# Rounded products for layer 0's xBC projection in a two-layer hybrid diffusion step, and what is moved around them

## The chip, the core and the metric

The kernel runs on one core of one Trainium2 chip. The metric is the device time of one execution in microseconds (us). Five engines work side by side: TensorE (PE; its weight loads are PEld), VectorE (DVE), ScalarE (ACT), GpSimd (POOL) and SyncE (SP), which issues the loads. Each works through its own list of instructions in order and waits only on semaphores.

## The reference, cut to what matters

128 context and 256 latent tokens (384 together) of width 1024 pass through two trunk layers. What the change touches is the first half of a layer: an RMS norm with a modulation, and one input projection whose columns go to attention A, attention B, a gate z, the part `xbc` (768 columns) and `dt` (16 columns, padded to 32).

```python
h = modulate(rmsnorm(x, n1), sh1, sc1)          # sh1, sc1 = slices of silu(c) @ w_ada + b_ada
a_q, a_k, a_v, b_q, b_k, b_v, z, xbc, dt_raw = jnp.split(h @ w_in, points, axis=-1)
xbc = jax.nn.silu(conv_centred(xbc, conv_w, conv_b))
dt = softplus(dt_raw + dt_bias)                  # the scan's decays come from dt
```

Then follow the two attentions, the state-space scan on xbc and dt, an output projection, and a mixture of 16 experts.

## The kernel before

Activations lie transposed, channels on partitions, in 8 chunks k of 128 channels by 384 tokens. Weights stream through a ring of 8 slots of 1 MB; SP issues their loads in one fixed order (`pieces`), and before each it waits until the slot's former piece is used up (`release`). The order of the work is written out by hand in `layer_steps`: every engine walks the same list of steps and does its own part of each.

**A product in parts.** A full fp32 product is one matmul in the source and two matmul records in the trace. A rounded product splits both operands into a high part (rounded to fp32r) and a low part (the rest) and sums three fp32r matmuls: high x high, high x low, low x high. ACT makes a high part by a copy, DVE the low part by a subtraction. The experts, the output projection, the row stage below and layer 1's xbc (`ROUNDED = (1,)`) work so; layer 0's xbc uses full fp32 products.

**Layer 0's front.** The modulation of layer 0 is not there yet, so its columns come in eight pieces `first(0..7)` of 1 MB. For each chunk j, PE multiplies (`first`, L755), ACT copies the result to `ada_rows` (L1572), PE turns it (`first_turn`, L766), and DVE adds the bias and gain (L1840, L1842) and modulates chunk j of the normalised x (L1903). Then PE multiplies chunk k of h with the six column blocks of xbc (L981). Within chunk k, PE does `first_turn(k + 1)` after block 1 and `first(k + 2)` after block 4. In chunks 3 and 7, four thin products for dt come first (L963); in chunk 7 DVE copies their sum to `tmp` (L2083; in a rounded layer it is L2088), and PE waits for that copy at `dt_rows` behind block 2 (L780).

**The pieces of xbc's weights** are ("xbc", l, 0) to ("xbc", l, 3), two chunks each. Where a layer is rounded, ACT makes `wx_hi` (`x_split`, L1425; two buffers, so pieces 2 and 3 wait until chunks 1 and 3 are multiplied) and DVE makes the rest in place (`x_rest_split`, L1938). The high part of h, `hT_hi`, lies over ring slots 2 and 3; in layer 0 those slots hold xbc pieces 1 and 0 first, and h is split late (`h_split`: ACT L1595, DVE L1943).

**Behind the front** comes the row stage: tokens by 512 columns (L1014), parts p = 0 to 5 of w_in, each split by ACT and DVE (`split_win`, L1416 and L1933). Beside it run the convolution (ACT L1607, DVE L2097 to L2102), Silu (L1620), dt's softplus on DVE (L2110 to L2142, which ends with `da_lo` and `dtd`), and `masked_rest(0)`: 16 ACT instructions at L1431 which need `da_lo`. They stand as step ("rest", 0) behind the Silus and before the first copies of row results (L1639, L1641). PE needs those copies to get its PSUM banks back.

**Layer 1's front** has three pieces of adaLN weights ahead of xbc (`early = 3`; PE L704) and three more behind the row stage (`burst`). DVE makes the rest of x's piece 1 before it scales x by the norm (L1862); `parts_of(c)` makes each chunk's fp32 form h_f (L1871) and its low part (L1876), ACT its high part (L1488).

## Time and profile before

| | |
|---|---|
| median of 3 runs | 789.55 us (788.98 to 789.73) |
| the profiled execution | 789.94 us, of which its span is 788.0 us |
| busy: PE, PEld, DVE, ACT, POOL | 742.7, 576.4, 582.8, 502.6, 50.4 us |
| layer 0's front, up to the row stage | 0 to 62.1 us |
| layer 0's row stage | 62.1 to about 135 us |
| layer 1's front, up to the row stage | about 406 to 444.7 us |

The page of the profile has busy times, the span in slices, the chain of work that ended last, and groups of instructions. A timeline's row has the start in us, the length in us, the engine, the source line, the operation, out<-in, shape and count, and in brackets the idle time before it and what ended it. Merged rows (x2, x16) run from the first start to the last end. A matmul's own length includes its drain, so the pace of a stream is read from a run of many.

### The profile page before, as it was taken

Reading aid. Unit: us, or ns where it says so; the run is one execution under the profiler, and the core shown is the slowest. Engines: PE = TensorE matmul, PEld = TensorE weight load, DVE = VectorE, ACT = ScalarE, POOL = GpSimd, SP = SyncE. Lnnn points to the kernel's source line nnn. Section 1 sums busy time; section 2 is a strip of 40 time slices with the busy share of each in tenths; the row PEclk is TensorE's granted clock in tenths of the full one; section 3 lists DMA queues with packets and bytes.
Section 4 is the critical chain, followed back from the end, with each engine's and each line's share of the span. In section 5 each row is a group of like instructions: output and inputs, shape, how many; then the busy total and the mean of one; then the engine's idle time right before and its main releaser. Section 6 shows DMA issues by size and latency. Waiting matters only on the chain.

```text
span 788.0 us, 10974 instructions
## 1 busy us (share of the span) xinstructions
PE 742.7 (94%) x4020; PEld 576.4 (73%) x4020; DVE 582.8 (74%) x968; ACT 502.6 (64%) x834; POOL 50.4 (6%) x36
## 2 busy tenths in 40 slices
PE   4999999899999999999989999989999999999994
PEld 2557777457976888888769888745698788888874
DVE  3258377886656889999868646869676789999965
ACT  3047784484466877777646488557556787777752
POOL 0001342000000000000000035200000000000000
PEclk9999999999999999999999999999999999999998
DMA  9963033978328899999843112386741189999902
GB/s 363 423 237 108 1 133 116 424 274 309 109 107 340 318 377 362 377 376 361 308 181 146 67 54 70 119 362 216 283 153 56 54 319 363 374 364 379 372 17 83
DMA packets 33489, 186.26 MB, mean 236 GB/s; under 512 B 5136, under 2 KB 6288, under 8 KB 16400
## 3 DMA queue, kind: packets, MB, share of 16 engines
q1 hardware_dynamic: 33424, 185.42, 62.4%
q8 instruction: 37, 0.61, 0.3%
q14 instruction: 28, 0.23, 0.1%
HBM read 182.79 MB, written 2.62 MB: 235 GB/s over the span
## 4 chain that ended last, share of the span: by engine, by line
PE 70%; DVE 13%; ACT 10%; issue 5%; DMA 1%; DVEq 0%; ACTq 0%; SPq 0%
PE psum L874 22%; PE psum L903 11%; PE psum L1014 7%; PE psum L1216 5%; PE psum L981 4%; PE psum L926 3%; PE psum L704 3%; PE psum L978 3%; PE psum L852 2%; DVE att L2250 1%; ACT ud L1431 1%; PE psum L755 1%; DVE xbc L2097 1%; ACT split L1407 1%; ACT ring_r L1416 1%
## 5 line engine op out<-in xcount | busy, mean ns | idle before, releaser
L2039 DVE TENSOR_TENSOR split<-ring,split 128x2048 fp32r<-128x2048 f32 x96 | 219.9, 2290 | 26.8 <-ACT split L1532 25.4
L1532 ACT CAST split<-ring 128x2048 fp32r<-128x2048 f32 x96 | 183.5, 1912 | 21.9 <-PE psum L903 14.5
L874 PE MATMUL psum<-split,y_hi 128*128 128x512 f32 x512 | 160.8, 395 | 0.4 <-ACT selT L1505 0.4
L874 PEld LDWEIGHTS psum<-split,y_hi 128*128 128x128 f32 x512 | 93.7, 188 | 18.6 <-issue 0.5
L874 PE MATMUL psum<-split,y_lo 128*128 128x512 f32 x256 | 100.1, 391 | 0.0
L1014 PE MATMUL psum<-ring_r,hT_hi 128*128 128x512 f32 x216 | 74.2, 398 | 1.4 <-ACT row L1641 1.4
L903 PE MATMUL psum<-split,hidT 128*128 128x512 f32 x256 | 69.7, 394 | 1.8 <-DVE hidT_lo L2044 1.8
L903 PEld LDWEIGHTS psum<-split,hidT 128*128 128x128 f32 x256 | 47.3, 188 | 14.2 <-DVE hidT_lo L2044 4.8
L874 PEld LDWEIGHTS psum<-split,y_lo 128*128 128x128 f32 x256 | 48.1, 188 | 10.2
L2480 POOL TENSOR_TENSOR ud<-const,da_hi 128x1024 fp32r<-128x1024 f32 x12 | 27.3, 2294 | 404.2 <-DVE da_lo L2141 397.3
L1014 PEld LDWEIGHTS psum<-ring_r,hT_hi 128*128 128x128 f32 x216 | 40.6, 191 | 10.9 <-issue 2.4
L1445 ACT ACTIVATE row<-xT 128x384 f32<-128x384 f32 x40 | 20.2, 520 | 32.8 <-DVE xT L1950 29.9
L1706 ACT ACTIVATE hT<-psum,att 128x384 f32<-128x384 f32 (+1 forms) x48 | 24.0, 507 | 26.7 <-DVE att L2260 18.6
L704 PE MATMUL psum<-ring,silu_c 128*32 128x512 f32 x320 | 39.9, 600 | 0.0
L903 PE MATMUL psum<-split,hidT_lo 128*128 128x512 f32 x128 | 39.5, 390 | 0.0
L1950 DVE SCALAR_TENSOR_TENSOR xT<-psum,mods,xT 128x128 f32<-128x128 f32 x64 | 23.7, 413 | 20.7 <-PE psum L1216 15.3
L981 PE MATMUL psum<-hT,ring 128*128 128x384 f32 x96 | 35.3, 502 | 0.0
L1216 PE MATMUL psum<-m_hi,split 128*128 128x384 f32 x128 | 34.4, 337 | 0.0
L1216 PE MATMUL psum<-o_hi,split 128*128 128x384 f32 x128 | 33.7, 336 | 0.0
L1538 ACT CAST hidT<-psum 128x256 fp32r<-128x256 f32 x32 | 12.0, 374 | 28.8 <-PE psum L887 28.8
L1014 PE MATMUL psum<-ring_r,hT_lo 128*128 128x512 f32 x72 | 28.8, 400 | 0.0
L1431 ACT ACTIVATE ud<-const,da_lo 128x128 fp32r<-128x128 f32 x96 | 28.7, 393 | 0.0
(308 smaller groups left out, 1431.5 us busy)
## 6 DMA issues: line engine op xcount, KB each, us to landing
ring<-in_w_gu SPq DMA_DIRECT2D x64, 1024.0 KB, 5.2
ring<-in_w_ada SPq DMA_DIRECT2D x40, 1024.0 KB, 6.9
ring<-in_w_down SPq DMA_DIRECT2D x32, 1024.0 KB, 5.3
ring<-in_w_rows SPq DMA_DIRECT2D x12, 1024.0 KB, 4.8
ring<-in_first SPq DMA_DIRECT2D x8, 1024.0 KB, 14.6
ring<-in_w_out SPq DMA_DIRECT2D x8, 1024.0 KB, 5.2
ring<-in_w_xbc SPq DMA_DIRECT2D x8, 800.0 KB, 8.3
par<-in_par SPq DMA_DIRECT2D x1, 1728.0 KB, 13.3
```

Source lines behind the costliest of these rows:

```text
L704: last = pe.matmul(psum[32 * q:32 * q + 32, 7, :], silu_c[:, k, :], w[:, q * 512:(q + 1) * 512], start=(k == 0), stop=(k == KD - 1), skip_ ...
L874: last = pe.matmul(dst, x[:, g, t, :], w[:, j, :], start=(t == 0 and i == 0), stop=(t == KD - 1 and i == 2))
L903: last = pe.matmul(psum[:, b, :], x, w[:, half * 512:(half + 1) * 512], start=(e % EPG == 0 and i == 0), stop=(e % EPG == EPG - 1 and i == ...
L981: last = pe.matmul(bank(("xbc", l, c))[:, 0:TOK], w[:, kk, c * P:(c + 1) * P], hT[:, k, :], start=(k == 0), stop=(k == KD - 1))
L1014: last = pe.matmul(dst, x[:, k, tok], w[:, j, :], start=(k == 0 and i == 0), stop=(k == KD - 1 and i == 2))
L1216: last = pe.matmul(dst[:, 0:TOK], w[:, k, cols], x[:, k, :], start=(part == 1 and k == 0 and i == 0), stop=(part == 0 and k == 3 and i == 2))
L1431: ins = act.activation(ud[:, 1, d, h, :], c_(tri), ACT.Copy, scale=da_lo[:, m, SH * d + h:SH * d + h + 1])
L1532: act.copy(splits[unit_split(n)][:, 0, :], slot(key)).then_inc(raised("whi", l, p), 1)
L1706: act.activation(probs[:, u % 8, 0:w], src[:, 0:w], ACT.Exp, bias=att[:, 1, u:u + 1], scale=SCALE, accum_out=att[:, 2, u:u + 1]).then_inc( ...
L1950: ins = stt(xT[:, c, part], src[:, part], mods[:, l, gate + c, j:j + 1], xT[:, c, part], ALU.mult, ALU.add)
L2039: tt(lo, slot(unit_key(l, p, n)), hi.bitcast(F32), ALU.subtract).then_inc(raised("wlo", l, p), 1)
L2480: ins = tt(ud[:, 0, d, :, :], c_(tri).unsqueeze(1).to_broadcast((P, SH, P)), da_hi[:, m, 8 * d:8 * d + 8].bitcast(F32).unsqueeze(2).to_bro ...
```

## The change

It does these things:

- `ROUNDED = (0, 1)`: layer 0's xbc becomes three fp32r matmuls per product too. Chunk 0 is done high-part-of-h first, so that it waits for `hT_hi` alone; this holds for layer 1 as well.
- In layer 0, ACT's loop over j now holds: copy `ada_rows`, wait for chunk j's h_f, make its high part, and behind j = 0, 2, 4 `x_split` of piece 1, 2, 3. `split_win(0, 0)` and `(0, 1)` come behind the whole loop instead of behind j = 6.
- In layer 0, DVE scales x in groups (1, 1, 2, 4 chunks), modulates into `h_f`, makes each low part at once, and `x_rest_split` behind chunks 0, 2, 4. The rests of `split_win(0, 0)` and `(0, 1)` come behind the whole loop. The copy of dt's sum to `tmp` now stands in step xbc, behind them.
- `hT_hi` has ring slots 2 and 3 from the start of layer 0, so six slots are left for the first pieces. By the slot rule the load of first 4 waits for first 0, xbc 2 for first 1, first 5 for first 2, first 6 for first 3, xbc 3 for first 4, and first 7 for first 5; the parameters `par`, which `tables()` on DVE needs behind chunk 5, are issued behind first 7.
- The norm's factor goes to its own tile `rstd` instead of back to PSUM.
- `masked_rest(0)` moves between Silu 2 and Silu 3, in both layers; DVE's rest of `split_win(l, 2)` moves from the middle of dt's chain to behind the convolution.
- Layer 1: `early = 4`, so one adaLN piece moves from the burst to ahead of xbc; x's rest 1 on DVE moves from before the scaling to behind chunk 1's parts.

```diff
-ROUNDED = (1,)
+ROUNDED = (0, 1)
...
-    early = 3 if l else 0
+    early = 4 if l else 0
...
-    s += [("rows", 0, m) for m in range(TILES)] + [("rest", 0)] + [("rows", 1, m) for m in range(TILES)]
+    s += [("rows", 0, m) for m in range(TILES)] + [("rows", 1, m) for m in range(TILES)]
...
-    burst = early + 3
+    burst = 6 if l else 3
...
+        if key in (("xbc", 0, 0), ("xbc", 0, 1)):
+            last_use[b] = pieces.index(("first", 0, 5)) + 0.1 * (key[2] + 1)
...
                                 if l in ROUNDED:
+                                    h = h_f
+                                    if k == 0:
+                                        pe.wait_ge(*hx("hx_hi", l, 0))
+                                        for c in range(6):
+                                            cols = slice(c * P, (c + 1) * P)
+                                            pe.wait_ge(*fill(("xbc", l, c)))
+                                            for n, wp in enumerate((wx_hi[:, 0, 0, cols], x_lo_of(l, 0)[:, 0, cols])):
+                                                pe.matmul(bank(("xbc", l, c))[:, 0:TOK], wp, hT_hi[:, 0, :], start=(n == 0), stop=False)
                                     pe.wait_ge(*hx("hx_lo", l, k))
-                                    h = h_f
...
                         if not (l or arg[0]):
                             act.wait_ge(setup_dve, 1)
+                            x_split(0, 0)
...
                                 act.copy(ada_rows[:, 0:2 * P], bank(key)[:, 0:2 * P]).then_inc(*was_read(key))
-                                if j == KD - 2:
-                                    for p in range(2):
-                                        split_win(0, p)
+                                act.wait_ge(*modulated(0, 0, j))
+                                act.copy(hT_hi[:, j, :], h_f[:, j, :]).then_inc(sig["hx_hi"], 1)
+                                if j in (0, 2, 4):
+                                    x_split(0, 1 + j // 2)
+                            for p in range(2):
+                                split_win(0, p)
...
                             act.activation(xbc[:, c, :], xbc[:, c, :], ACT.Silu).then_inc(sig["xbc_silu"], 1)
+                            if c == 2:
+                                act.wait_ge(sig["da_lo"], per["da_lo"] * l + 1)
+                                masked_rest(0)
...
+                if not l:
+                    groups = {0: (0, 1), 1: (1, 2), 2: (2, 4), 4: (4, KD)}
+                    scaled(0, 1).then_inc(dve_step, 1)
+                    dve.wait_ge(dve_step, dve_steps())
+                    for c in range(KD):
+                        first(c)
+                        moved(c).then_inc(sig["h"], 1)
+                        if c + 1 in groups:
+                            scaled(*groups[c + 1]).then_inc(dve_step, 1)
+                            dve.wait_ge(dve_step, dve_steps())
+                        dve.wait_ge(*modulated(0, 0, c))
+                        rest_of(c)
+                        if c in (0, 2, 4):
+                            x_rest_split(0, 1 + c // 2)
+                        if c == KD - 3:
+                            tables()
+                    for p in range(2):
+                        split_win(0, p)
+                    return
                 if l in ROUNDED:
...
                     parts_of(1)
+                    x_rest_split(l, 1)
                     parts_of(2)
...
-                        split_win(l, 2)
                         dve.wait_ge(sig["dt_r"], per["dt_r"] * l + 1)
...
                         for c in range(3, 6):
                             side_taps(c)
+                        split_win(l, 2)
                         split_win(l, 3)
```

## Rows read from the trace of the kernel before

**Rows 1.** The page, part 1: busy us, share of the span, instructions.

```profile
PE 742.7 (94%) x4020; PEld 576.4 (73%) x4020; DVE 582.8 (74%) x968; ACT 502.6 (64%) x834; POOL 50.4 (6%) x36
```

**Rows 2.** The chain of waits in layer 0: start us, us, what.

```profile
20.07 2.04 PE psum L981 x6
...
27.63 1.00 PE psum L755 x16
...
56.83 0.83 PE psum L963 x8
...
125.25 8.20 PE psum L1014 x36
```

**Rows 3.** The chain of waits in layer 1.

```profile
426.74 12.79 PE psum L978 x72
...
515.83 2.71 PE psum L704 x24
```

**Rows 4.** Timeline of PE in layer 0.

```profile
19.57 0.50 PE L766 MATMUL psum<-pcol,ada_rows 128*128 128x2 f32 x4
...
59.58 0.74 PE L780 MATMUL psum<-pcol,tmp 128*128 128x16 f32 x6
...
62.14 0.47 PE L1014 MATMUL psum<-w_hi,hT_hi 128*128 128x512 f32 x1
```

**Rows 5.** Loads: SP's issue of xbc 1, its time to landing, and that of w_in's parts.

```profile
5.09 0.47 SPq L1323 DMA_DIRECT2D ring<-in_w_xbc  x1
...
ring<-in_w_xbc SPq DMA_DIRECT2D x1, 800.0 KB, 16.0
...
ring<-in_w_rows SPq DMA_DIRECT2D x12, 1024.0 KB, 4.8
```

**Rows 6.** Timeline of ACT in both layers.

```profile
15.62 0.37 ACT L1572 COPY ada_rows<-psum 128x256 f32<-128x256 f32 x1 [0.43 <-PE psum L755]
...
46.49 3.70 ACT L1416 CAST w_hi<-ring 128x2048 fp32r<-128x2048 f32 x2
...
76.63 4.79 ACT L1431 ACTIVATE ud<-const,da_lo 128x128 fp32r<-128x128 f32 x16
...
422.93 1.48 ACT L1425 CAST wx_hi<-ring 128x1536 fp32r<-128x1536 f32 x1 [0.44 <-PE psum L978]
```

**Rows 7.** Timeline of DVE in both layers' fronts.

```profile
25.63 0.16 DVE L1840 TENSOR_TENSOR mods<-psum,pcol 128x4 f32<-128x4 f32 x1 [3.65 <-PE psum L766]
...
26.09 0.67 DVE L1903 TENSOR_SCALAR hT<-hT,amul,mods 128x128 f32<-128x128 f32 x2
...
49.78 4.48 DVE L1933 TENSOR_TENSOR ring_r<-ring,w_hi 128x2048 fp32r<-128x2048 f32 x2
...
57.68 0.56 DVE L2083 COPY tmp<-psum 128x384 f32<-128x384 f32 x1 [0.70 <-PE psum L963]
...
409.96 1.76 DVE L1938 TENSOR_TENSOR ring_r<-ring,wx_hi 128x1536 fp32r<-128x1536 f32 x1 [3.43 <-issue]
...
413.86 0.95 DVE L1862 TENSOR_TENSOR hT<-xT,psum 128x768 f32<-128x768 f32 x1
...
417.08 1.75 DVE L1862 TENSOR_TENSOR hT<-xT,psum 128x1536 f32<-128x1536 f32 x1
```

**Rows 8.** Timeline of PE around layer 0's first row copies.

```profile
82.08 0.70 PE L1014 MATMUL psum<-ring_r,hT_hi 128*128 128x512 f32 x2 [1.12 <-ACT row L1641]
...
86.28 0.61 PE L1014 MATMUL psum<-w_hi,hT_hi 128*128 128x512 f32 x1
```

**Rows 9.** Timeline of PE in layer 1, around xbc's start and the row copies.

```profile
414.20 0.47 PE L978 MATMUL psum<-hT_hi,wx_hi 128*128 128x384 f32 x1 [3.08 <-DVE hT_lo L1876]
...
463.80 0.71 PE L1014 MATMUL psum<-ring_r,hT_hi 128*128 128x512 f32 x2 [0.28 <-ACT row L1641]
```

**Rows 10.** By windows: busy PE, PEld, DVE, ACT, POOL; granted clock; DMA.

```profile
80.00:85.00 5.00, 3.88 (x18) 3.18 (x18) 0.81 (x7) 5.00 (x17) 1.17 (x2) 0.83 0.00 0
...
415.00:420.00 5.00, 4.74 (x19) 4.42 (x19) 4.89 (x11) 2.85 (x7) 0.00 (x0) 0.72 0.22 92
```

More of the change, by code:

```diff
@@ L294, in build @@
                     pieces.append(("first", 0, 0))
-                for i in range(2 if l in ROUNDED else 0, KD // 2):
+                for i in range(2 if l else 0, KD // 2):
                     pieces.append(("xbc", l, i))
@@ L301, in build @@
             elif s[0] == "ada":
-                if s[2:] == (1, 0) and l in ROUNDED:
+                if s[2:] == (1, 0) and l:
                     pieces += [("xbc", l, 0), ("xbc", l, 1)]
@@ L357, in build @@
         last_use[b], last_key[b] = n, key
-    more_slots = [b for b in range(HELD, RING) if b not in [place["xbc", l, i] for l in ROUNDED for i in range(2)]]
+        if key in (("xbc", 0, 0), ("xbc", 0, 1)):
+            last_use[b] = pieces.index(("first", 0, 5)) + 0.1 * (key[2] + 1)
+    more_slots = [b for b in range(HELD, RING) if b not in [place["xbc", l, i] for l in ROUNDED if l for i in range(2)]]
     for l in range(DEPTH):
@@ L384, in build @@
         wx_hi = sb("wx_hi", [P, 2, 2, XBC], F32R)
+        rstd = sb("rstd", [P, TOK])
         with ExitStack() as shared:
@@ L971, in _ @@
                                 for c in range(6):
-                                    if k == 0:
+                                    if k == 0 and l not in ROUNDED:
                                         pe.wait_ge(*fill(("xbc", l, c)))
@@ L976, in _ @@
                                         hi, lo = wx_hi[:, i % 2, kk, cols], x_lo_of(l, i)[:, kk, cols]
-                                        for n, (wp, hp) in enumerate(((hi, hT_hi), (hi, hT_lo), (lo, hT_hi))):
+                                        for n, (wp, hp) in enumerate(((hi, hT_lo), (hi, hT_hi), (lo, hT_hi))[0:3 if k else 1]):
                                             last = pe.matmul(bank(("xbc", l, c))[:, 0:TOK], wp, hp[:, k, :],
-                                                             start=(k == 0 and n == 0), stop=(k == KD - 1 and n == 2))
+                                                             start=False, stop=(k == KD - 1 and n == 2))
                                     else:
@@ L1421, in x_split @@
                 if i == 2:
-                    act.wait_ge(sig["wx_spent"], ROUNDED.index(l) + 1)
+                    act.wait_ge(sig["wx_spent"], per["wx_spent"] * ROUNDED.index(l) + 1)
                 elif i == 3:
@@ L1476, in norm @@
                 act.wait_ge(act_step, act_steps())
-                act.activation(src[:, 0:TOK], src[:, 0:TOK], ACT.Exp, scale=-0.5).then_inc(sig["rstd"], 1)
-                if l not in ROUNDED:
+                if l in ROUNDED:
+                    act.activation(rstd, src[:, 0:TOK], ACT.Exp, scale=-0.5).then_inc(*was_read(key))
+                else:
+                    act.activation(src[:, 0:TOK], src[:, 0:TOK], ACT.Exp, scale=-0.5).then_inc(sig["rstd"], 1)
+                if l != 1:
                     return
@@ L1582, in _ @@
                             split_win(l, arg[0])
-                        if l in ROUNDED and arg[0] == 0:
+                        if l and arg[0] == 0:
                             x_split(l, 3)
@@ L1848, in norm @@
                 key = ("ss", l, n)
+                if not l:
+                    x_rest_split(0, 0)
                 if l in ROUNDED:
-                    x_rest_split(l, 1)
-                dve.wait_ge(sig["rstd"], l + 1)
-                dve.wait_ge(*full(key))
+                    dve.wait_ge(*taken(key))
+                else:
+                    dve.wait_ge(sig["rstd"], l + 1 - sum(1 for x in ROUNDED if x < l))
+                    dve.wait_ge(*full(key))
                 if l == DEPTH:
@@ L1891, in norm @@
                     return
-                for c0, c1 in ((0, 1), (1, KD)):
-                    ins = scaled(c0, c1)
-                    if c1 == KD:
-                        ins.then_inc(*was_read(key))
-                        dve.wait_ge(*taken(key))
-                    else:
-                        ins.then_inc(dve_step, 1)
-                        dve.wait_ge(dve_step, dve_steps())
-                    for c in range(c0, c1):
-                        first(c)
-                        for j, part in ((0, slice(0, P)), (1, slice(P, TOK))):
-                            ins = ts(hT[:, c, part], hT[:, c, part], amul[:, l, n, c, j:j + 1],
-                                     mods[:, l, SH1 + c, j:j + 1], ALU.mult, ALU.add)
-                        ins.then_inc(sig["h"], 1)
-                        if c == KD - 3:
-                            tables()
-                        if c == KD - 2:
-                            for p in range(2):
-                                split_win(0, p)
             def tables():
@@ L2074, in _ @@
                             split_win(l, arg[0])
-                        if l in ROUNDED and arg[0] == 0:
+                        if l and arg[0] == 0:
                             x_rest_split(l, 3)
```

40 lines of the change are left out of this document (20 added, 20 removed).

## The prediction

> **What bounds the kernel now.** I read the page first: PE is busy 94% of the span [rows 1], so in general a change is worth what it takes off PE, or adds there as waiting. The question in each stage is whether PE is really held by its own work. In layer 0's front the chain of waits alternates between products of xbc, `first` and `first_turn`, all on PE and back to back: six records (three fp32 products) take 2.04 us, `first` 1.00 [rows 2]. Every other engine is ahead of it. That is the cover under which the change works. In layer 1 the same product, rounded, runs at 12.79/72 = 0.178 us per matmul [rows 3], 0.53 us for three, against 2.04/3 = 0.68. The loads show next what can hold PE up: xbc 1, issued at 5.1, lands 16.0 us later, at 21.1 [rows 5]. The timelines of ACT and DVE give the durations [rows 6, 7], and that of PE shows the places which the moved steps aim at [rows 8, 9].
>
> **Layer 0's products.** 48 products lose 0.68 - 0.53 = 0.15 us each: 7.2 us, if PE stayed the bound. It doesn't, I think, because each chunk now needs a chain through three engines. With the durations: on ACT copy 0.37, x_split 1.48, a split of w_in half of 3.70, and a cast of 384 columns 0.50 (between 0.37 for 256 and 1.48 for 1536) [rows 6]; on DVE 1.1 from the end of a turn to the end of modulating (25.63 to 26.76), 0.95 and 1.75 for scaling two and four chunks, 1.7 a rest of x, 2.2 a rest of w_in, and 0.56 for a pass over 384 columns, as the copy of dt's sum or a low part [rows 7]. A hand-over costs 0.05 to 0.1. I mark the walk by T(j), the end of `first_turn(j)`.
>
> T(1). Behind chunk 0's high part ACT does `x_split(0, 1)`, which waits for xbc 1: 21.1 to 22.7. Only then comes the copy of `first(1)`, 23.1, and PE's turn, 23.5. It was 20.07 (19.57 + 0.50) [rows 4]. So the front starts **3.4 us late**, and the same x_rest keeps DVE until 24.5.
>
> T(2). DVE modulates chunk 1 (25.6), scales two chunks (26.6), makes the low part (27.1); PE starts chunk 1 at 27.2, two blocks 1.07, turn: T(2) = 28.6. Chunk 1 ends at 31.8 (four blocks 2.14, `first(3)` 1.0).
>
> T(3). ACT's `x_split(0, 2)` needs the end of chunk 1: 31.9 to 33.4; copy 33.8; T(3) = 34.2, about 1 us of waiting for PE. DVE's rest of x runs to 35.2, modulate 36.3, scale four chunks 38.0, low part 38.6. PE starts chunk 3 at 38.7, 1.3 us late; dt's thin products 0.83 [rows 2], two blocks: T(4) = 40.9.
>
> T(5), T(6). The same pattern with x_split 3 behind the end of chunk 3 (44.1): T(5) = 46.5. `par` is issued only behind first 7, at about 43.7. A 1 MB load alone needs 4.8 us, par is 1.7 times that behind it, so it lands at about 52.5, and `tables()` holds DVE till 53.5 [rows 5]. T(6) is 51.4 by then; chunk 6's low part comes at 55.9 and T(7) = 57.4. It was 54.1. **The loop as a whole gives nothing back**: 3.4 us late at T(1), 3.3 at T(7).
>
> The wait at `dt_rows`. PE starts chunk 7 at 59.9, when its low part is there, and reaches `dt_rows` 0.83 + 1.6 us later: 62.3. It needs DVE's copy of dt's sum. That now stands behind both rests of w_in, and these wait for ACT's splits, which come behind its whole loop: ACT's last high part ends at 59.2, split 61.0; DVE rest 0 63.3, rest 1 65.5, copy 66.05. So PE **waits 3.8 us** in chunk 7. In the kernel before, the copy started 0.70 us after DVE fell idle, as soon as the sum was there [rows 7], and `dt_rows` came at 59.58 with no wait [rows 4]. Then 0.6 and three blocks: the row stage starts at 68.3, not 62.14 [rows 4]: **+6.2 us**. Walking the kernel before in the same way gives 61.9, so the walk's own error is some tenths.
>
> **masked_rest and the rests.** The 16 instructions take 4.79 us on ACT [rows 6], right ahead of the row copies for which PE waits 1.12 us in layer 0 and 0.28 in layer 1 [rows 8, 9]. Moved between the Silus, they run while DVE does the convolution. The copies then come 3.7 us before PE wants them, so only the waits go: -1.1 and -0.3. Once PE is back at 82.08, its next 12 matmuls take until 86.28 [rows 8], 4.2 us instead of 12 x 8.20/36 = 2.7 [rows 2]: **-1.5 us** if that goes too. The granted clock is 0.83 in that stretch, a mix of the levels 1.2 and 2.4 GHz, and it falls again, to 0.72, behind the wait of 3.08 us in layer 1 [rows 9, 10]: 5 us at 0.72 are 1.4 us of full clock lost. The new wait at `dt_rows` is longer than either, so I set **+1.5 us** for it, and this pair cancels. The Trainium skill speaks against the change here: "TensorE: Matmul & The Clock Gate", section "HAM oscillation", says that a wait between bursts of matmuls throttles the array, and the next burst starts at half rate. By that rule the new wait costs twice; were it wrong here, the sum below would be 1.5 us lower. The move of DVE's rest of `split_win(l, 2)` (2.2 us) costs nothing: the row stage wants part 2 some 19 us after its start.
>
> **Layer 1.** PE waits 3.08 us for chunk 0's low part at 414.20 [rows 9]. x's rest 1 (1.76) no longer stands before the scaling, and the high part suffices; but `hT_hi` now lies where the fourth early adaLN piece was read, and PE ends that one (2.71/3 = 0.9 us [rows 3]) at about 412.0, so ACT's high part is ready at 413.15: 1.05 us earlier. Then DVE becomes the bound. Its list, by the durations above: low part 0 413.7, scale two 414.7, chunk 1 415.8, rest of x 1 417.4, chunk 2 418.6, scale four 420.2, chunks 3 and 4 422.6; ACT's last four high parts (some 0.9 each, an estimate from two passes like the 384-wide one) end at 423.9 and its x_split 2 at 425.4; DVE's rest 2 427.1, chunks 5 to 7 430.6, w_in's rest 432.8, rest 3 434.6. PE began chunk 6, which needs it, at 439.53 - 18 x 0.178 = 436.3 [rows 3]: **-1.7 us**. Bounds: -1.0 by the start alone, -2.6 if no wait is left. The burst behind the row stage, on the chain itself, has two adaLN pieces instead of three: **-0.9 us**. Its load sits in slot 2, which is free, so I cost it at nothing. `rstd` in its own tile costs nothing: its scaling is bound by columns, and one end still reads xT.
>
> **The sum.** +6.2 - 1.1 - 1.5 + 1.5 - 0.3 - 1.7 - 0.9 = +2.2 us. Everything behind the front hangs on PE, and the experts' loads are not late, so I carry it to the end. The profiled execution would take 789.94 + 2.2 = 792.1; the median of the runs lies 0.4 us lower, so 791.8. I say **791.8 us**. A measurement of this kernel tells about 0.2% (1.6 us) from no change; +0.3% is little more.
>
> **The rivals.**
> - **The front stays with PE** (faster). For it: in layer 1, with the same split of labour, the last 72 rounded matmuls before dt's products run without a wait [rows 3]. If ACT and DVE keep up in the loop, the 7.2 us are gained there, and the late start (3.4) and `dt_rows` (3.8) are paid: nothing is lost at the row stage, and 2.2 - 6.2 = -4.0 is left: 785.6 us. Against it: layer 1 has its splits of w_in and x's parts made ahead. It decides if x_split 1 lands by about 19, or the waits at T(3) and T(5) are hidden. Chance 0.25.
> - **Same time.** The walk is 1 to 2 us too dark in the front, or the clock doesn't fall at `dt_rows`: 790. Chance 0.2.
> - **Half pace in the loop as well** (slower, further out). PE waits 1 to 2 us some five times in the front; if the pace falls behind two more of these, as behind the 1.12 us of [rows 8], that is 2 x 1.5 more: 794.8. Chance 0.12.
> - **Only one half works**: the products bring nothing since the loads bind with six slots. The walk has xbc 3 landing at 41 and first 7 at 48.2, both before they are wanted, so this needs loads 3 us later than the rows say; it is inside the former.
>
> My forecast, +2 with its parts, has 0.43. Slower by over 0.2% is 0.43 + 0.12 = 0.55, within it 0.2, faster 0.25. The range: down to 785, which takes in the faster rival but not one in which the late start or the wait at `dt_rows` vanishes too; up to 796 for the half pace.
>
> **What the changed profile would show.** Right: `first_turn(1)` near 23 with PE waiting for ACT; PE waiting about 3.8 us for DVE's copy before `dt_rows`, and both rests of w_in just ahead of that copy; the row stage from about 68; no wait at the first row copies; ACT's masked rest between Silus; xbc's end in layer 1 1.5 to 2 us earlier relative to its sums. Wrong: the row stage before 64 (then the front stayed with PE), or a `tmp` copy that starts within 1 us of dt's sum.

## The result, and the profile after

The changed kernel took **797.25 us** in the median of eight runs (794.49 to 801.02), the kernel before 789.57 in eight on the same chip: a ratio of 1.0097, with a 95% interval of 1.0080 to 1.0115. It is 7.7 us slower. I had forecast 791.8, within 785 to 796: the sign was right, the size was not, and the range did not hold it.

The profiled execution took 794.49 us, the shortest of the eight. Two things have to be explained: the 4.7 us between the two traces (spans of 792.7 and 788.0), and 2.8 us that the median of the changed kernel lies above its own trace, where that of before lay 0.4 below.

First the page, part 1, of the changed kernel. PE is busy 4.8 us less than in [rows 1], and the span is longer: the rounding did take work off PE, and more than that came back as waiting.

```profile
PE 737.9 (93%) x4067; PEld 582.8 (74%) x4068; DVE 591.1 (75%) x979; ACT 509.5 (64%) x844; POOL 50.4 (6%) x36
```

The chain of waits in layer 0's front (start us, us, what). In [rows 2] it was PE and nothing else.

```profile
4.86 16.05 DMA ring<-in_w_xbc
20.93 1.47 ACT wx_hi L1436
22.40 0.28 ACT ada_rows L1584
...
22.82 0.65 PE psum L770 x4
23.47 1.17 PE psum L989 x3
24.64 1.86 PE psum L759 x16
...
31.90 1.49 ACT wx_hi L1436
33.41 1.76 DVE ring_r L1965
...
44.09 9.84 DMA par<-in_par
53.94 0.18 DVE nsink L1948
...
61.83 1.85 DVE ring_r L1960
...
64.04 2.28 DVE ring_r L1960
66.32 0.48 DVE tmp L2115
...
66.94 0.86 PE psum L784 x6
67.80 3.07 PE psum L989 x9
```

The reader sees the forecast's walk, nearly step for step: the second turn (now L770) ends at 23.47, behind the load and ACT's split; `par` holds the tables; both rests of w_in (L1960) stand ahead of DVE's copy, and behind them PE makes `dt_rows` (L784). What PE waited for in the first 75 us:

```profile
PE psum L770 <- ACT ada_rows L1584: 4.7, 4, 2.2
PE psum L784 <- DVE tmp L2115: 3.6, 1, 3.6
```

The nine products behind that wait took 3.07 us, at half pace. Behind the wait of 2.2 us ahead of the second turn, `first` (L759) took 1.86 us, where [rows 2] had 1.00. By windows (columns as in [rows 10]) the granted clock is low behind both waits, and no longer low at 80 us and at 415 us, where [rows 10] had 0.83 and 0.72:

```profile
20.00:25.00 5.00, 2.75 (x16) 1.79 (x18) 2.49 (x5) 1.74 (x2) 0.00 (x0) 0.82 1.01 419
...
65.00:70.00 5.00, 3.06 (x13) 3.09 (x14) 4.89 (x13) 3.41 (x9) 0.00 (x0) 0.76 0.02 5
80.00:85.00 5.00, 5.00 (x24) 4.14 (x23) 2.51 (x2) 4.29 (x8) 0.00 (x0) 1.00 0.52 210
415.00:420.00 5.00, 4.38 (x34) 1.12 (x33) 1.61 (x4) 1.48 (x4) 0.00 (x0) 1.00 0.41 136
```

Then the chain between the end of layer 0 and the row stage of layer 1:

```profile
399.87 11.34 PE psum L930 x64
411.21 0.69 issue
411.90 0.88 PE psum L741 x2
412.78 0.65 PE psum L744 x2
413.43 1.64 issue
415.07 0.80 PE psum L744 x2
415.87 3.62 PE psum L708 x32
...
419.56 0.99 ACT hT_hi L1499 x2
```

In the middle of layer 1's sums PE stands still for 1.64 us, waiting for nothing that the profile shows ("issue"). The trace before has no such pause there: its longest "issue" behind 80 us is 0.7 us.

Where the two traces part (us from the span's start, and how late the changed kernel is):

| | before | after | later by |
|---|---|---|---|
| first product of layer 0's row stage | 62.14 | 70.67 | 8.5 |
| products behind the first row copies | 82.08 | 89.53 | 7.5 |
| first combining product of layer 0's experts | 394.41 | 399.87 | 5.5 |
| ACT's first high part in layer 1 | 412.30 | 419.56 | 7.3 |
| layer 1's row stage | 444.72 | 450.62 | 5.9 |
| span | 788.0 | 792.7 | 4.7 |

### The profile page after: what moved, and what is told of

Same layout as the page of the kernel before. It is cut to its first block, busy times and chain, and to the rows that moved or that the text cites. A ratio compares the mean times of both kernels' runs of the same rounds, so it can differ in the third digit from the quotient of the medians.

```text
span 792.7 us, 11088 instructions
## 1 busy us (share of the span) xinstructions
PE 737.9 (93%) x4067; PEld 582.8 (74%) x4068; DVE 591.1 (75%) x979; ACT 509.5 (64%) x844; POOL 50.4 (6%) x36
## 4 chain that ended last, share of the span: by engine, by line
PE 70%; DVE 12%; ACT 9%; issue 5%; DMA 3%; SPq 1%; ACTq 0%; DVEq 0%
PE psum L878 22%; PE psum L1025 11%; PE psum L907 11%; PE psum L1227 5%; PE psum L708 3%; PE psum L930 3%; PE psum L856 2%; DMA ring<-in_w_xbc 2%; PE psum L989 2%; DVE att L2277 1%; DMA par<-in_par 1%; ACT split L1418 1%; PE psum L1095 1%; PE psum L891 1%; PE psum L1109 1%
## 5 line engine op out<-in xcount | busy, mean ns | idle before, releaser
L989 PE MATMUL psum<-hT_lo,wx_hi 128*128 128x384 f32 x96 | 34.3, 375 | 1.4 <-DVE ring_r L1965 0.8
L989 PE MATMUL psum<-hT_hi,ring_r 128*128 128x384 f32 x84 | 28.8, 343 | 0.0
```

Source lines behind the costliest of these rows:

```text
L989: last = pe.matmul(bank(("xbc", l, c))[:, 0:TOK], wp, hp[:, k, :], start=False, stop=(k == KD - 1 and n == 2))
```

## The experiments

The theories. **A**: the time is lost in the new hand-overs from ACT to DVE to PE in layer 0's front. **B**: falls of the granted clock behind the new waits cost the rest, and in some executions more than in the profiled one. **C**: PE's stall at layer 1's sums comes from the place of its instructions in their stream. The products that some kernels add are read by nobody.

### The changed kernel again

No edit.

> The changed kernel unaltered, for its spread and its granted clock on the same chip as the next kernels. All theories: 794.5 to 801 us, median near 797. Theory A (new hand-overs between ACT, DVE and PE in layer 0's front) and theory B (falls of the granted clock behind those waits) both expect its profile to show the row stage of layer 0 starting at 70 to 71 us of the span; B alone expects that its runs differ by their mean granted clock (0.986 to 0.993) and that every run with the lower clock is the longer one. Theory C (stalls in which PE waits for nothing that the profile shows) expects one such stall of over 1 us in layer 1's front again, at the same instruction.

Measured: 797.51 us (795.43 to 798.79), ratio 1.0104 (1.0091 to 1.0117). The row stage started at 70.2 and the stall was there, 1.25 us. The clock and the time go together: the thirteen runs of this kernel had mean granted clocks of 0.993 (794.5 and 794.7 us) to 0.985 and 0.986 (798.5 to 801.0); the order is not strict in between. The repeat's trace shows one such place: one and the same stretch, first in the changed kernel's profile, then in this one.

```profile
530.00:535.00 5.00, 2.76 (x22) 1.95 (x22) 4.67 (x15) 2.35 (x12) 0.00 (x0) 1.00 1.02 429
535.00:540.00 5.00, 4.07 (x35) 2.08 (x33) 4.76 (x17) 3.12 (x14) 0.00 (x0) 1.00 0.90 357
```

```profile
530.00:535.00 5.00, 3.93 (x26) 2.47 (x30) 4.72 (x14) 2.08 (x11) 0.00 (x0) 0.69 1.01 424
535.00:540.00 5.00, 5.00 (x28) 2.33 (x26) 3.13 (x12) 1.65 (x7) 0.00 (x0) 0.63 0.94 336
```

PE's pauses ahead of the fall are the same in both, first after, then the repeat:

```profile
530.52 0.49 PE L1158 MATMUL psum<-qkT 64*128 64x128 f32 x4 [1.04 <-ACT hT L1724]
531.68 0.63 PE L721 MATMUL psum<-const,ada_rows 128*128 128x128 f32 x4 [0.30 <-ACT ada_rows L1404]
```

```profile
529.94 0.49 PE L1158 MATMUL psum<-qkT 64*128 64x128 f32 x4 [1.03 <-ACT hT L1724]
531.10 0.63 PE L721 MATMUL psum<-const,ada_rows 128*128 128x128 f32 x4 [0.30 <-ACT ada_rows L1404]
```

The same pauses of 1.03 and 0.30 us came with a fall towards 1.2 GHz in one execution and with none in another. The fall takes (0.31 + 0.37) x 5 = 3.4 us of full clock, but not as much time: the repeat is 0.58 us ahead at the first of these rows (529.94 against 530.52) and 1.21 behind at 545.4 (546.57 against 545.36), so that it cost 1.8 us there. The rest fell into time in which PE would have waited anyway. Of the eighteen traces of these experiments nine show a fall between 520 and 540 us and seven one between 230 and 270; the traces before and after show neither.

That time and clock go together isn't true of every kernel. The kernel before has the same pauses (1.03 us at 525.90, 0.30 at 527.06), and its runs beside these experiments differ in clock too, but hardly in time: the 30 runs with a clock of 0.990 or less have a median of 789.95 us, the 17 with 0.995 one of 789.80, and the 32 between them one of 789.13.

### The two halves of the change

The rest of the change alone, on the kernel before: `ROUNDED` stays `(1,)`, the other parts are made.

```diff
-    early = 3 if l else 0
+    early = 4 if l else 0
-... + [("rest", 0)] + ...
+                            if c == 2:
+                                masked_rest(0)
...
```

> The kernel before with all parts of the change but layer 0's rounded product: the masked rest beside the convolution, the rest split of in_w later, four pieces of adaLN early in layer 1 with a burst up to six, layer 1's first product with the high part first, rstd in its own tile. Theory A (front of layer 0 holds the whole loss): these parts gain what the prediction gave them, 1.1 + 0.3 (masked rest) + 1.5 (the pause at 82 us) + 0.9 (burst) and nothing in layer 1's front: 786 to 787 against 789.6. By the prediction's own terms, with layer 1's front 1.7 more: 784.1. Theory C (layer 1's front has lost by a stall or by the fourth early piece): 788 to 790.

Measured: **783.07 us** (782.45 to 785.42), ratio 0.9926 (0.9913 to 0.9939). These parts gain 6.4, not the 5.5 of the forecast's terms, and more than any of the three expectations. Layer 1 has no stall here:

```profile
402.96 1.29 PE psum L741 x4
404.25 3.62 PE psum L705 x32
...
407.94 0.99 ACT hT_hi L1496 x2
```

The rounding nearly alone: the changed kernel with `early = 3` and its burst, the step `("rest", 0)` and the place of `split_win(l, 2)` put back. Layer 1's first product with the high part first, the later place of x's rest 1 and `rstd` stay as in the changed kernel, so these are in this half and in the other as well.

> The kernel before with layer 0's rounded product alone: the changed kernel with the masked rest, the split of in_w's third part, and layer 1's early pieces and burst put back. If the two halves of the change add up: 789.5 plus the 14.4 by which the changed kernel (797.5) is above the rest of the change alone (783.1), that is 803.9. By the prediction's terms (late start, wait for the dt rows, half pace; 3.4 + 3.8 + 1.5, and less the pause at 82 us that a later DVE would lengthen) it would be 798. If the row stage hides part of the late start behind the masked rest, which then binds less: 799 to 801.

Measured: 795.88 us (794.65 to 799.26), ratio 1.0080 (1.0061 to 1.0099). All three expectations were too high. The halves don't add up: +6.2 and -6.4 would make no change at all, and together they are 7.7 slower. What both halves hold is counted twice in this; it can't be the whole, since layer 1's part with its burst is worth 3.0 (below). The chain shows another reason, for the row stage: with the front late, PE runs on its own work and never waits for the row copies, masked rest moved or not.

```profile
71.27 17.47 PE psum L1025 x72
88.74 0.44 PE psum L1062 x4
```

So the late start and the masked rest were the same microseconds: who pays the one doesn't pay the other. Layer 1's front also goes the other way on top of the rounding. From the first combining product to ACT's first high part it took 18.05 us here (402.81 to 420.86) and 19.69 in the changed kernel: 0.86 for the fourth early piece, a stall 0.35 longer, and a gap ahead of the sums 0.42 longer.

The rest of the change in two parts, on the kernel before: first the row stage's alone, then all but it.

> The kernel before with the row stage's part alone: the masked rest beside the convolution and the split of in_w's third part later, in both layers. The prediction gave it 1.1 + 1.5 in layer 0 and 0.3 in layer 1: 786.7. If the rest of the change's gain (6.4 in all) lies here and not in layer 1's front: 785.

> The kernel with the rest of the change alone, less the row stage's part: layer 1's early pieces, its burst, the first product with the high part first, rstd in a tile. The prediction gave it 1.7 + 0.9: 787. If what layer 1's front gained was the pause and the fall of the clock at 410 to 420 us (0.94 and 0.72): 786. If both parts add up with the run before it, the two gains make 6.4.

Measured: 786.26 us (785.31 to 788.55), ratio 0.9956 (0.9943 to 0.9969), and 786.83 (785.38 to 791.35), 0.9969 (0.9954 to 0.9984). Against 789.80 beside them that is 3.5 and 3.0, where the forecast's terms had 2.9 and 2.6, and together 6.5, where both in one kernel gained 6.4. The terms of the gains were right to 0.6 us. The first keeps the low clock in layer 1, the second the one at 80 us; in each the fall is gone behind the pause that was shortened.

### The hand-overs of layer 0's front

DVE's copy first:

```diff
+                    dve.wait_ge(*full(("dtT", 0)))
+                    dve.tensor_copy(tmp[:, 0, 0:TOK], ...)
                     for p in range(2):
                         split_win(0, p)
...
```

> DVE's copy of the dt rows out of the bank comes ahead of its two rests of in_w instead of behind them. Theory A: PE's wait for it (3.59 us) shrinks to below 0.5 and the rests move behind, where the first row tile takes them late by about 1 us: 3 us faster than the changed kernel, near 794. Theory B: with the wait goes the half pace of the nine products behind it (3.07 us against 1.6), 1.4 more, and the spread of the runs shrinks: 4.5 to 6 faster, near 792. Theory C: 0 to 1 faster, the wait is replaced by PE's own stalls. A theory that the loads of six ring slots bind: no gain.

Measured: 795.10 us (792.99 to 797.51), 2.4 less than the changed kernel beside it and 1.1 above theory A's number. The wait at `dt_rows` is gone and another is in its place, the next thing that is late. PE's wait in the first 75 us:

```profile
PE psum L1025 <- DVE dtw L2139: 2.7, 1, 2.7
```

The first row tile needs the bank that held the dt rows, and DVE reads it behind both rests and the first side taps.

The x weights' splits later as well. DVE's rests come behind chunks 1, 3 and 5. ACT's first split comes behind the high part of chunk 1, the other two between the copy of `first` and the high part of chunks 3 and 5:

```diff
+                                if j in (3, 5):
+                                    x_split(0, (j + 1) // 2)
...
-                                if j in (0, 2, 4):
-                                    x_split(0, 1 + j // 2)
+                                if j == 1:
+                                    x_split(0, 1)
...
-                        if c in (0, 2, 4):
+                        if c in (1, 3, 5):
```

> As the kernel with the copy first (795.1), and the splits of the x weights one step later in the loop; the small parameters are loaded where the changed kernel loads them. Against the mended front (788.6) it tells what the early load is worth. Theory A with the hand-overs alone: 789 to 789.5. If the load of the parameters binds (in the changed kernel it landed at 53.9 us and DVE's tables, the seventh chunk and the rest waited for it): 791 to 793.

Measured: 791.03 us (788.39 to 794.98), 4.1 below the last. The load of the parameters does bind: it landed at 48.7 us, PE waited 2.2 us ahead of a `first`, and the nine products behind took 3.37 us. With `if n == RING:` it is issued at 18.7 instead:

> As the kernel with the copy first, and ScalarE's and VectorE's splits of the x weights one step later in the loop over chunks, so that the modulated chunks are handed over ahead of them, and the small parameters are loaded with the ninth piece of the ring. Theory A: of the late start and loop (3.4 us) 1.5 to 2.5 come back beyond the copy's 4.5: 789 to 790.5. Theory B: the same, and the runs' spread falls below 0.4%. Loads bind: no better than the kernel with the copy first, 792.

Measured: 788.60 us (785.57 to 791.45), ratio 0.9984 (0.9970 to 0.9999). Theory A's number came out, 0.4 better: 8.9 below the changed kernel. Where PE doesn't wait, a chunk of the loop now takes 4.8 us from turn to turn, where the plain products took 5.5. The spread did not shrink (B's 0.4% was 0.7%).

The rests ahead of the last chunk (ACT's and DVE's `split_win(0, 0)` before the last hand-over; the side taps behind the read of the bank):

> On the mended front: in_w's first high part and its rest go ahead of the last chunk of the loop, and DVE reads the dt bank before it adds the first side taps. In the mended front PE waited 2.7 us at its first row tile for that read. Theory A: the wait falls below 0.5 and the row stage starts near 60.5 us of the span instead of 62.9: 2.4 faster than the mended front, near 786. Theory B: with the wait go the falls of the granted clock in 60 to 70 us (0.84 and 0.82), 0.8 to 1 more: near 785.2. Theory C (PE's stall at layer 1's sums, 1.3 to 1.6 us in every kernel with layer 0 rounded and in none without): the stall stays, so the kernel with the rest of the change alone (783.1) is not beaten.

Measured: 785.40 us (784.30 to 788.76), as expected, and not for the reason given. The wait had only moved: DVE made the rest ahead of the last chunk's modulation.

```profile
PE psum L974 <- DVE hT_lo L1905: 2.5, 1, 2.5
```

The row stage started at 62.6, as in the mended front (62.9), not at 60.5. What went was the low clock between 60 and 70 us (0.84 and 0.82 in the mended front, 1.0 here), some 1.7 us. The two traces are 2.0 apart at layer 0's experts; where the rest of the 3.2 us in the medians comes from is not shown.

Then the order in which the next engine needs things: copy, first rest alone, read of the bank, and only then the second rest, which the row stage wants 36 products later, some 8 us.

```diff
-                    for p in range(2):
-                        split_win(0, p)
+                    split_win(0, 0)
...
+                        if not l:
+                            split_win(0, 1)
+                            side_taps(0)
                         side_taps(1)
```

> On the mended front (788.6): after the copy of the dt rows DVE makes the rest of in_w's first part alone (the first three row tiles read no other), reads the dt bank, and only then makes the second rest and the first side taps. Nothing is moved ahead of the loop's last chunk, as it was in the kernel with the rests hidden, where the wait only moved to that chunk (2.5 us). Theory A: PE's wait of 2.7 us at the first row tile falls below 0.3, the row stage starts near 60.3 us. Theory B: the half pace behind that wait goes too, 0.8 more. Both: 785 to 786. If the second rest, now later, holds up the side taps and so the banks of the second and third row tile: 788.

> The kernel that reads first again, beside the kernel with three early pieces: 781.5 to 782.5, below the rest of the change alone (783.1), so that layer 0's rounded product is worth 1 to 1.5 us once its hand-overs are in order.

Measured: 781.67 us (781.48 to 782.50) with a ratio of 0.9902 (0.9888 to 0.9916), and when repeated 783.68 (781.47 to 785.25), 0.9931 (0.9917 to 0.9945). The first was better than expected, the second 1.2 above what was expected of it; 781.5 to 782.5 are the runs with a clock of 0.996 and more. PE no longer waits at the first row tile, which starts at 57.6 us. The second rest (L1963) and the side taps behind it hold up the second tile, by 0.2 us:

```profile
56.86 2.28 DVE ring_r L1963
...
60.71 13.85 PE psum L1025 x60
```

Part of this is the clock. The front up to the second turn has the same order of work here, in the mended front and in the next kernel. That turn starts at 20.5 us in this trace, with a clock of 1.00, and at 22.9 in the mended front's, where the clock was 0.76. In the next kernel's trace, again with 0.76, the row stage starts at 60.1. So 2.5 of the 5.3 us by which the row stage is earlier than in the mended front (57.6 against 62.9) are clock, and not the order of DVE's work.

The first combining product of layer 0 starts at 387.0 here and at 390.3 in the rest of the change alone: the rounded product does gain 3.3 us in its layer once the hand-overs are in order and the clock stays up. When repeated it was 2.9 (387.44); in the trace of the next kernel, the same in layer 0 but with the low clock in the front, 0.7 (389.61). At ACT's first high part of layer 1 it is 1.3 (406.60 against 407.94). Layer 1's sums, with stalls of 0.79 and 1.44 us, have taken the rest back.

In whole times the two kernels (783.07 and 781.67 or 783.68) can't be told apart by these runs.

Three early pieces of adaLN instead of four, on that kernel:

> The kernel that reads first (781.7) with three pieces of adaLN ahead of layer 1's front instead of four, as in the kernel before. In the changed kernel ACT's first modulated chunk of layer 1 starts only when the fourth piece is done (0.86 to 0.9 us later, 1.3 with its wait), and the burst behind the row stage is one piece (0.9) shorter. If both are on the path: 781.3, the same within 0.2%. If the fourth piece is hidden beside DVE's and ACT's rounding after all: 782.5.

Measured: 783.22 us (781.72 to 785.05), the same as 783.68 beside it. In the trace the pieces take 2.76 instead of 3.62 us on the chain ahead of ACT's first high part. The fourth piece isn't hidden there, and is given back in the burst, which takes 2.71 us with three pieces early and 1.85 with four: it is moved, not saved.

### The clock and the stall

Products where PE waits, in the changed kernel:

```diff
+                                    if l == 0 and c == 1 and k == 0:
+                                        for _ in range(12):
+                                            pe.matmul(bank(("dtT", 0))[:, 0:TOK], ...)
...
             def dt_rows(l):
 
+                if not l:
+                    keep(("keep_dt", l), 16, 7)
```

> The changed kernel with products that nobody reads, put where PE waits: 12 (128x384) ahead of the second turn of layer 0's front and 16 (128x512) ahead of the dt rows. They change no wait of another engine. Theory B: the granted clock stays at 1.0 in 20 to 30 us and in 65 to 75 us, the nine products behind the dt rows take 1.6 us instead of 3.07, the row stage starts 1.5 to 2.5 earlier, and the runs' spread (794.5 to 801) shrinks: 794 to 795.5. Theory A alone (the clock does not matter): no change, or 0.5 slower where the products outlast the wait: 797 to 798.

Measured: **790.87 us** (789.05 to 795.07), ratio 1.0020 (1.0005 to 1.0035): 6.6 less than the repeat of the changed kernel, with twenty-eight products more and every hand-over as late as before. It is more than theory B had asked for. The clock in the front, by windows:

```profile
20.00:25.00 5.00, 4.82 (x33) 4.47 (x35) 2.15 (x4) 1.74 (x2) 0.00 (x0) 1.00 1.01 418
65.00:70.00 5.00, 4.87 (x28) 3.50 (x27) 4.89 (x12) 3.57 (x9) 0.00 (x0) 1.00 0.00 0
```

and the chain there: the nine products are back at full pace, the row stage starts 1.2 us earlier (1.5 to 2.5 were expected).

```profile
63.67 3.40 PE psum L729 x15
...
67.20 0.81 PE psum L786 x6
68.01 1.67 PE psum L991 x9
69.68 5.47 PE psum L1031 x24
```

Two more things had changed, which I hadn't foreseen: the stall at layer 1's sums was gone, and ten of twelve runs had a clock of 0.994 or more. So the 6.6 us are three effects, and two runs were to separate them. They lengthen PE's stream and leave the waits in layer 0's front as they are; what they do fill is most of PE's first wait, ahead of the first sums (2.6 us are left of 9.6 with 14 of them):

```diff
             pe.wait_ge(setup_dve, 1)
+            for _ in range(14):
+                pe.matmul(psum[:, 7, 0:2], ones, ones[:, 0:2], ...)
             sums(0, 0)
```

> The changed kernel and 28 products of two columns ahead of the first sums; at 0.21 us each (measured with 96 of them) they take 6 of the 9.6 us that PE waits there, so that they delay nothing. They lengthen PE's program by as many products as the kernel kept busy had, without filling any of its pauses. Theory C: the stall at layer 1's sums (1.25 to 1.64 us) is gone or has moved, 1.3 to 1.6 faster than the changed kernel if gone: 796. Theory B: the falls of the clock stay, so the time stays above 795; if it came near the 790.9 of the kernel kept busy, B would fall.

> The changed kernel and the same 14 products. With 28 of them the stall was gone, but they outlasted PE's first wait and layer 0 began 2 us late. Theory C: the stall (1.64 us in the changed kernel's profile) is gone, and nothing is late. Theory B in its strong form (falls of the clock in layer 0's front are what brings the later falls, at 250 and 530 us): the front's falls stay and so do the later ones, 795.5 to 796 in the median. In its weak form (whether PE's later pauses cost a fall is a matter of where they lie, and any shift of the program can change it): 792.5 to 794.5.

Measured: 794.55 us (791.96 to 795.23) with 28, although they outlasted PE's first wait and layer 0 ran 2.2 us late, and **793.04** (790.85 to 794.36) with 14, ratio 1.0038 (1.0024 to 1.0053). The expectations for 28 had taken 0.21 us for one product; that is one of its two records. In both the stall is gone. The timeline of the latter:

```profile
411.59 0.88 PE L741 MATMUL psum<-row,ones 128*128 128x384 f32 x2 [0.24 <-issue]
412.31 1.45 PE L744 MATMUL psum<-row,ones 128*128 128x384 f32 x4
413.69 3.64 PE L708 MATMUL psum<-ring,silu_c 128*32 128x512 f32 x32
```

From the first combining product (400.01) to ACT's first high part (417.45) it is 17.4 us, against 19.7 in the changed kernel: the stall and the longer gap ahead of the sums cost 2.2. The median fell by 4.2 to 4.5. The 2 us more are most likely falls of the clock that came less often (the runs had 0.987 to 0.992), while those of the front stayed. That speaks for B's weak form, that any shift of the program can change whether a pause costs a fall; the busier start is a rival that no run separates. The products in the two waits of layer 0's front are worth 2.2 us beyond this (793.04 against 790.87).

The 96 such products, on the rest of the change alone:

> The kernel with the rest of the change alone (783.1), and 96 products of two columns ahead of the first sums, in the 9.7 us in which PE waits for DVE anyway. They lengthen PE's program by as many products as the rounding adds in layer 0's loop. Theory C, that the stall at layer 1's sums comes from the place of PE's instructions in their stream: the stall of 1.3 to 1.6 us appears at the same line or near it, and the time is 784.3 to 784.7. If the stall comes from the later arrival of layer 0's end or from the transfers beside it: no stall, 783.1.

Measured: 816.14 us (814.71 to 817.60), a miss: I had taken a product of two columns for almost free. It is two records with a weight load each, and takes 0.43 us.

```profile
1.12 41.12 PE psum L746 x192
```

No stall came at the sums either. But the 96 products are 191 records more in the page (4211 against 4020), and the rounding adds 47 (4067). So this run shows that a longer stream need not bring a stall; whether one longer by 47 records would, without the rounding, was not tested. Over all traces it stands so: all ten with layer 0 rounded and nothing added have a stall at layer 1's sums, and the five with layer 0 rounded and products added ahead of them have none there. Nor have the five without layer 0's rounding.

Both remedies on the kernel that reads first:

> As the kernel that reads first, and eight products (f32, 64 columns) that nobody reads in the three pauses of 0.4 to 0.6 us around the first turn of layer 0, behind which the mended fronts showed a granted clock of 0.73 to 0.76 in 20 to 25 us and took 3.88 us for twelve products that take 2.1 at full pace. Theory B: 1.0 in that stretch, 1.5 to 1.8 faster than the kernel that reads first, near 783.7, and fewer later falls, so a spread below 0.3%. Theory A alone: the same time, or 0.3 slower.

> The kernel that reads first (781.7), and 14 products of two columns ahead of the first sums; one took 0.43 us with 96 of them, so 14 take 6 of the 9.6 us in which PE waits there. They add 28 product and 28 load instructions to PE's stream, as the kernel kept busy did. Theory C: the stalls at layer 1's sums (0.79 and 1.44 us in the kernel that reads first) are gone or moved: 779.5 to 780.3 if gone. If the stall hangs on something else: 781.7 and the same stall.

Measured: 783.21 us (781.45 to 783.67), ratio 0.9913 (0.9900 to 0.9925), and 782.05 (779.86 to 782.25), 0.9891 (0.9877 to 0.9905). The first tells nothing on filling the pauses: both traces of the kernel it was made from had no low clock in that stretch to begin with. It tells something on the stall, though: with eight products more there is none at layer 1's sums, and one at the last sums of the kernel, 370 us further on and longer (2.5 us), the only one of over 0.8 us behind the first 80 us.

```profile
PE psum L741 <- issue: 2.7, 2, 2.5
```

In the second the stalls are gone, but the median is not the 779.5 to 780.3 that were expected then. The profiled execution had a granted clock of 0.74 in 20 to 25 us; the two runs at 0.996 took 779.9 and 780.1, the three at 0.993 782.1. Its ratio is the lowest of all, but its interval overlaps that of the kernel it came from.

## Why the prediction was wrong in size, and where it was right

**Layer 0's front** was right. T(1) 23.47 (forecast 23.5), `dt_rows` waiting 3.59 (3.8), the half pace behind it 1.4 (1.5). The row stage came 8.5 us late; 6.2 + 1.5 were forecast. The 0.8 more is the load of `par`: it took 9.8 us and landed at 53.9, not 52.5, and the last turn ended at 58.29, not 57.4. "The loop gives nothing back" held too, and this step of it mattered more than I gave it: loading `par` early is worth 2.4 (791.03 against 788.60).

**The row stage** was right: the pause at 82.08 and its low clock went, 2.6 forecast, 3.0 of the lateness gone by the experts (8.5 to 5.5). But I booked it to the masked rest. The kernel with the rounding and the masked rest put back shows that the late front ends that wait by itself.

**"Layer 1: -1.7 us"** is the term of the sum that failed in the trace, and the first failed step. The lateness grew from 5.5 to 5.9 instead of falling to 3.8. The steps of that walk hold: in the rest of the change alone ACT's first high part to the row stage takes 31.1 us, in the changed kernel too (419.56 to 450.62). What came on top is ahead of it: the stall of 1.64 us and a gap of 0.69 ahead of the sums, where the shifted kernel has 0.24, worth 2.2 by that run. Without them the lateness would be 3.7, and the term -1.8. No row of the trace before showed such a stall, and I had costed PE's longer stream at nothing without saying so. What the stall is stays open.

**Waits and burst** (-0.3, -0.9) were right: from 5.9 to 4.7.

**From the profiled execution to the median.** I wrote that the median lies 0.4 below the profile and subtracted it. In the changed kernel it lies 2.8 above. That is the second failed step: I priced the falls of the clock only where a new wait stands, and took PE's old pauses, behind which the trace showed a full clock, as safe. They aren't. In the same kernel one execution has a fall at 530 us, which costs 1.8 us, and another has none; and over thirteen runs the time goes with the clock. This is an inference from clocks and times, since of the thirteen runs only those of 794.49 and 795.43 us were traced. Why the kernel before doesn't pay in the same way, at clocks of 0.989 to 0.995, stays open. Together: 791.8 + 2.2 + 2.8 + 0.4 = 797.2.

**The rivals.** Half pace in the loop (794.8) came once in the profiled execution and not twice more: behind T(1), with 0.82 and 0.84 from 20 to 30 us and `first` at 1.86 us; from 30 to 65 us the clock was 1.0. It is a matter of the execution: with the copy first it was 0.50 and 0.82 from 25 to 35 us. The front staying with PE (785.6) is what the mended kernels come near to, with 781.7 to 788.6.

The Trainium skill's section "HAM oscillation" ("TensorE: Matmul & The Clock Gate"), that a wait between bursts costs the next burst at half rate, agrees with the 3.07 us behind `dt_rows`. Shorter pauses come with a fall as well, but not each time: behind the same pauses of 0.4 to 0.6 us the clock in 20 to 25 us was 0.76 in the mended front and 1.0 in the kernel that reads first.

**What stays open.** Why a given pause costs a fall in one execution and not in the next, and what exactly PE waits for in the stall. The page of the profile shows a queue of instructions beside the data:

```profile
q8 instruction: 37, 0.61, 0.3%
```

That is 37 transfers of 16 KB each. The Trainium skill, "Runtime: NRT & Kernel Launch", section "Instruction fetch mechanics", describes refills of an engine's instructions in blocks of 16 KiB and calls their cost mostly hidden. The size agrees. The count decides nothing: it is 37 in the kernel before too, which has no stall. That the stall is a refill which was not hidden is an inference that no run here tested, since they could only change where it falls, not what it is.

## What to carry to other kernels

When work is taken off the engine that bounds, order the work of the others by who waits for it: what the next engine needs first is done first, and a split that is wanted 8 us later goes behind it. The same rounded product cost 14 us (797.5 against 783.1) or nothing, by this order, one load, and the clock, whose share of the 14 us was not separated. After removing a wait look at once for what is late next (copy, then bank, then last chunk), and don't add up parts that hide behind the same lateness. Where a kernel has many short pauses on PE, read the granted clock of several executions before trusting one profile, and look once for pauses in which an engine waits for nothing.

## What the hardware showed that I had not expected

- Twenty-eight products that nobody reads made the kernel 6.6 us faster (797.5 to 790.9). Products that fill no wait in layer 0's front gave 4.5 of it.
- A fall of the granted clock is not fixed by the program: pauses of 1.03 and 0.30 us came with 1.00 in one execution and with 0.69 and 0.63 over 10 us in another. Of the 3.4 us of full clock in this, 1.8 were lost in time.
- A lower clock need not show in the time: the kernel before took 789.95 us at 0.990 and less, and 789.80 at 0.995.
- PE can stand still 1.25 to 1.83 us at one place, waiting for nothing that the profile shows, in all ten traces of kernels that round layer 0 and add no products. 8 products of 64 columns at the start moved that stall by 370 us, and 14 of two columns took it away.
- A float32 product of two columns cost 0.43 us in a stream of 96. Its weight loads kept PEld busy throughout, but that they set the pace isn't shown: the four records of a turn, of two columns too, take 0.50 us together.
